# The end of a hybrid gMLP and differential-attention layer: output tiles in six PSUM banks issued ahead of the last block's transposes

## The reference, cut to what matters

```python
h = rms_norm(x, norm_w) * (1 + scale(c)) + shift(c)
u_a, v_a, z_a, q_b, k_b, v_b, z_b = split(h @ w_in)           # 7 x 512 columns
a_out = u_a * (tril(w_s) @ rms_norm(v_a) + b_s) * silu(z_a)   # chunks of 128 positions, 4 groups
q, k = rope(rms_norm(q_b)), rope(rms_norm(k_b))               # 8 heads of 64
o = (softmax(q1 @ k1.T) - lam * softmax(q2 @ k2.T)) @ v_b     # causal, 4 head pairs, v of 128
b_out = rms_norm(o, subln_w) * (1 - lam_init) * silu(z_b)
x = x + gate(c) * (concat(a_out, b_out) @ w_out)              # (2048, 1024) per core
```

## Time and profile before

| | us |
|---|---|
| median of 3 runs | 522.16 |
| lowest, highest of the 3 | 520.88, 527.08 |
| the profiled execution, its own time | 526.04 |
| its span, the slowest core (core 4) | 524.6 |
| spans of the other cores | 514.8 to 523.1 |

### The profile page before, as it was taken

How to read it: one execution, slowest core, us unless ns; L and a number is a source line. 1 busy time by engine, 2 the same in 40 slices (tenths; PEclk the granted TensorE clock), 3 DMA queues, 4 the chain that set the end, 5 groups by cost and what they waited for, 6 DMA issues and landing times.

```text
span 524.6 us, 9798 instructions; the slowest of 8 cores (514.8 to 524.6 us)
## 1 busy us (share of the span) xinstructions
PE 445.6 (85%) x3104; PEld 217.6 (41%) x3104; DVE 334.7 (64%) x761; ACT 299.2 (57%) x402; POOL 88.6 (17%) x118
## 2 busy tenths in 40 slices
PE   0037679899999999999998999979997999999396
PEld 0002224344443444444445555445554555555242
DVE  1246732682775468888873767788558757868732
ACT  1066456545554227777767666666778778677100
POOL 1113440000671000000001112222222222122100
PEclk9997869899999999999999999979998999999879
DMA  8999978007624300021021122194140131011013
GB/s 200 251 308 257 311 240 180 0 1 131 167 87 139 121 1 2 1 47 36 1 81 41 42 81 60 62 282 202 47 156 2 39 100 67 22 62 42 40 63 139
DMA packets 15606, 53.90 MB, mean 103 GB/s; under 512 B 2242, under 2 KB 2626, under 8 KB 14660
## 3 DMA queue, kind: packets, MB, share of 16 engines
q1 hardware_dynamic: 13924, 45.36, 26.0%
q0 software_dynamic: 1152, 7.50, 8.3%
q10 hardware_dynamic: 480, 0.41, 0.3%
HBM read 50.29 MB, written 8.39 MB: 112 GB/s over the span
## 4 chain that ended last, share of the span: by engine, by line
PE 60%; DVE 11%; DMA 9%; issue 7%; ACT 6%; POOL 5%; DVEq 0%; SPq 0%; ACTq 0%; POOLq 0%
PE psum L647 15%; PE psum L470 13%; PE psum L1049 8%; PE psum L927 7%; DMA sb_WO<-w_adaT 5%; PE psum L897 5%; ACT sb_cs L910 3%; DMA sb_kT<-xT 3%; PE psum L1015 3%; POOL sb_cs L915 3%; DVE sb_F L984 3%; DVE sb_F L943 1%; PE psum L677 1%; PE psum L675 1%; PE psum L667 1%
## 5 line engine op out<-in xcount | busy, mean ns | idle before, releaser
L910 ACT ACTIVATE sb_cs<-psum,sb_small 128x1024 bf16<-128x1024 f32 x144 | 150.9, 1113 | 58.6 <-PE psum L897 55.2
L927 PE MATMUL psum<-sb_vB,sb_cs 128*128 128x129 bf16 x1088 | 89.5, 226 | 9.7 <-DVE sb_F L943 5.2
L927 PEld LDWEIGHTS psum<-sb_vB,sb_cs 128*128 128x128 bf16 x1088 | 64.4, 100 | 40.5 <-issue 40.1
L470 PE MATMUL psum<-sb_W,sb_hT 128*128 128x512 bf16 x256 | 65.8, 420 | 17.5 <-ACT sb_hT L466 15.4
L915 POOL TENSOR_TENSOR sb_cs<-sb_cs,sb_constb 128x256 bf16<-128x256 bf16 x64 | 44.5, 697 | 213.3 <-ACT sb_cs L910 208.7
L647 PE MATMUL psum<-sb_hT,sb_W 128*128 128x512 bf16 x280 | 65.8, 379 | 0.0
L897 PE MATMUL psum<-sb_qT,sb_kT 64*128 64x256 bf16 (+1 forms) x576 | 56.4, 274 | 6.9 <-ACT sb_cs L910 4.7
L470 PEld LDWEIGHTS psum<-sb_W,sb_hT 128*128 128x128 bf16 x256 | 26.4, 105 | 56.2 <-issue 34.1
L357 DVE SCALAR_TENSOR_TENSOR sb_F<-sb_WO,sb_F 128x1024 f32<-128x1024 f32 x24 | 30.2, 1257 | 30.5 <-DMA sb_WO<-w_adaT 22.0
L647 PEld LDWEIGHTS psum<-sb_hT,sb_W 128*128 128x128 bf16 x280 | 27.3, 98 | 30.0
L436 PE MATMUL psum<-sb_vnA,sb_constb 128*128 128x512 bf16 x32 | 11.9, 507 | 30.5 <-ACT sb_vnA L429 30.5
(11 more groups left out here) (114 smaller groups left out, 548.4 us busy)
## 6 DMA issues: line engine op xcount, KB each, us to landing
sb_WO<-w_adaT SPq DMA_DIRECT2D x24, 512.0 KB, 8.1
sb_W<-w_in POOLq DMA_DIRECT2D x5, 1024.0 KB, 9.9
sb_W<-x SPq DMA_DIRECT2D x8, 512.0 KB, 4.4
sb_cs<-w_out SPq DMA_DIRECT2D x8, 512.0 KB, 3.4
sb_hT<-x SPq DMA_DIRECT2D x8, 512.0 KB, 12.0
out<-sb_hT SPq DMA_DIRECT2D x8, 512.0 KB, 2.6
out<-sb_W SPq DMA_DIRECT2D x6, 512.0 KB, 2.8
sb_qT<-xT SPq DMA_DIRECT2D x4, 512.0 KB, 23.4
```

Of the source, the lines that this page charges most:

```text
L470: pe(lambda E: E.matmul(PS(bank), lhsT=hT[:, kc, 128 * tt:128 * (tt + 1)], rhs=wsl[slot][:, kc, :], start=(kc == 0), stop=(kc == KC - 1)), ...
L910: act(lambda E: E.activation(out=et, in_=psum[:, X:X + 2, :], func=AF.Exp, bias=negM, scale=0.125), reads=[pb[X], pb[Y], b_lam], writes=[b ...
L927: pe(lambda E, u=u, j=j, c=c, i=i: E.matmul(psum[:, j, 256 * c:256 * c + 129], lhsT=et[:, c, QB * u + 128 * j:QB * u + 128 * (j + 1)], rhs ...
```

## The change

It replaces the closing loop. First the one waiting post is recorded. The list of banks becomes [2, 3, 4, 5, 6, 7, 0, 1]. The tasks of block 3 are recorded down to its last fin_head, until its transposes stand at the front of fillq. They are taken out, and the six output tiles that are left of earlier blocks are recorded on TensorE, in banks 2 to 7. Only then come the transposes, in bank 0. The posts follow in this order: those of the first three of the six tiles, the two copies of the transposes, those of the other three. The four tiles of block 3 follow in banks 1, 2, 3 and 4, two by two with their posts as before. The number of operations of each kind and the stores are as they were; nothing is added or left out.

```diff
@@ -1131,7 +1131,7 @@
     def fill_one():
         it = fillq.pop(0)
         kind, run, wt = it[0:3]
-        bank = FB[fb_ctr[0] % 2]
+        bank = FB[fb_ctr[0] % len(FB)]
         fb_ctr[0] += 1
         posts.append(run(bank))
         if kind == "u":
@@ -1176,18 +1176,32 @@
             fill_one()
         if (last or (gs > 0 and jq >= 6 and kp == 3)) and fillq and len(posts) < 2:
             fill_one()
-    s = NS + 1
-    while due or fillq or posts or taskq:
-        now[0] = s
-        run_posts()
+    now[0] = NS
+    run_posts()
+    FB[:] = [2, 3, 4, 5, 6, 7, 0, 1]
+    fb_ctr[0] = 0
+    while not (fillq and fillq[0][0] == "tr"):
         while taskq:
             taskq.pop(0)()
-            run_due(s)
-        run_due(s)
+        run_due(10 ** 9)
+    tr = fillq.pop(0)
+    lead = min(6, len(fillq))
+    for k in range(lead):
+        fill_one()
+    early = posts[0:3]
+    rest = posts[3:]
+    del posts[:]
+    fillq.insert(0, tr)
+    fill_one()
+    for fn in early + posts + rest:
+        fn()
+    del posts[:]
+    run_due(10 ** 9)
+    while fillq or posts:
+        run_posts()
         for k in range(2):
-            if len(posts) < 2 and fillq:
+            if fillq:
                 fill_one()
-        s += 1
 
     P.emit()
     for bb in b_xr:
```

## The result

| | before | after |
|---|---|---|
| median, us | 523.13 (4 runs, 520.88 to 527.08) | 513.11 (4 runs, 512.21 to 514.7) |
| ratio to before, 95% interval | | 0.984 (0.980 to 0.988) |
| profiled execution: own time, span | 526.04, 524.6 | 513.64, 512.6 |

The medians and ratios from here on leave out executions in which one die (cores 0 to 3 or 4 to 7) ran longer at a lower granted clock.

A forecast was written before the change was run, and what follows sets the result against it. The prediction took TensorE's 6.79 us hole before block 3's transposes, plus slow matmuls behind it, as the bound. An ending 9.4 us earlier, less 0.5 for stores, takes 8.9 off 522.16: 513.3 us, range 510.0 to 517.0.

The forecast's parts named there:

- Idle time and TensorE's order: Ahead of block 3's transposes: six tiles take 10.38 us without bank waits, ending at 502.21; the 6.79 us hole disappears.
- The chain on VectorE: Block 3's add, squares, norm and eight L984 on VectorE keep their order and end at 498.64 in both versions.
- First on VectorE: The change's phrase for block 3's chain on VectorE; claimed to move nothing, only the TensorE work beside it moves.
- The start of the ladder: Block 3's first add, opening the closing adds and stores, starts at 505.61 instead of 515.01, set by VectorE, not TensorE.
- core 4's rows may stand for all: All cores do the same work, so the slowest, core 4 at 524.6 us, was taken to represent all eight.
- The stores: At the end, stores come closer together and delay the first half-tile store by 0 to 1.7 us; 0.5 was taken.
- One of its own signs of being wrong: In the closing adds and stores: the first store taking over 3 us would show the prediction wrong.
- the second rival: Closing stores queue up fully, first one 1.7 us late instead of 0.5: gain 7.7, time 514.5 us; chance 0.06.
- The clock: Behind the end of attention TensorE stays at 2.4 GHz throughout; 0.81 over two tiles would cost 0.7 us.
- The first rival: Granted clock 0.81 from the start of the tail: gain 6.5 us, time 515.7 us; chance 0.15.
- The total: Whole kernel: gain 8.9 us off the 522.16 us median gives 513.3 us, 1.7% less; chance 0.61.
- The fifth rival: Clock falls to 1.2 GHz at the end of attention and stays there: slower than before, 523.8 us; chance 0.03.

The follow-up runs named there:

- Experiment 1: Kernel before plus 28 throwaway matmuls filling the idle time ahead of block 3's transposes, six tiles left behind them: 518.03 us, ratio 0.996 to the kernel before.
- experiment 6: Changed kernel with all six adds behind the copies of the transposes instead of three ahead of them: 517.87 us in a single execution, tail 29.1 us.
- experiment 7: Changed kernel with own buffers for second halves, five tiles ahead, four adds ahead of the copies; timed twice: 509.83 and 511.34 us, ratios 0.978 and 0.980.
- lead2: Changed kernel with two tiles ahead of the transposes instead of six: 516.84 us, ratio 0.992 to the kernel before.
- halves: Changed kernel with a separate buffer and semaphore for the second half of each of the last two row tiles: 510.34 us, ratio 0.981 to the kernel before.
- best_again: Second timing of the changed kernel with own buffers for second halves, five tiles ahead and four adds ahead of the copies: 511.34 us, ratio 0.980.

## Why the prediction was right

**Idle time and TensorE's order.** Right. Six tiles fit into the hole with no wait for a bank, and the transposes start 12.05 us behind the copies L943 (502.21 - 490.15 = 12.06 by the sum). Experiment 1 gives the idle time 5.2 us and the clock 2.5 of the 7.7 us.

**The chain on VectorE.** Right: 8.49 us in both. "First on VectorE" moved nothing.

**The start of the ladder.** The first add of block 3 started at 499.37 + 2.67 - 0.69 = 501.35, which is 15.61 us behind the copies, against 15.46 by the sum. VectorE set it, as forecast, and experiment 6 showed so. The 0.15 is the step between adds, 0.66 us here (2.67 for four) and not 0.60. The term of this step, a ladder that starts 9.4 us earlier, measured 24.86 - 15.61 = 9.25 against core 4 of the kernel before. But "core 4's rows may stand for all" was not quite so. Its ladder starts latest of the eight and is the shortest: 24.86 and 7.11 us, where the medians are 24.3 and 7.6. By the medians the ladder starts 8.7 us earlier. The sum of start and ladder is about the same (31.97 against 31.9), so the forecast lost nothing by it. One slip has no effect either: behind block 3's first tile only three are left, not four, so TensorE ends at about 510.2 by the prediction's own rows and not at 511, which is the 20.07 us measured.

**The stores.** This is the term that was mis-sized. From the first add's start to the last one's end the ladder took 510.10 - 501.35 = 8.75 us instead of 7.11. So 1.6 us were lost on these two cores, and 8.6 - 7.6 = 1.0 us in the medians of the eight, where the prediction took 0.5; its upper bound was 1.7. One of its own signs of being wrong came true here: the first store of the ladder took 3.4 us to land, against 2.0 before, and over 3 us was the sign. The two waits of adds were to be 2.2 us each and were 3.52 and 2.55, and TensorE ended 4.3 us ahead of the last add instead of 2. The prediction preferred the low end because a store 2.1 us behind a 512 KB one had taken 2.01 us all the same. Here two 512 KB stores are issued 2.0 and 0.6 us ahead of it (at 500.14 and 501.55, the ladder's about 502.1), and the DMA engines are busy nearly all the time until 504.5 (core 2; columns as before):

```profile
501.00:504.50 3.50, 3.50 (x18) 1.57 (x16) 1.04 (x2) 0.00 (x0) 0.00 (x0) 1.00 0.93 366
```

Over the same stretch the share is 0.92 to 0.93 on the other seven cores. Experiment 4 takes these two stores out, and 1.1 us come back. That is the mechanism of the second rival, which had a chance of 0.06 and a gain of 7.7 us. The gain in the tail is 9.25 - 1.64 = 7.6 us, 7.7 in the medians, and not 8.9; it is 7.5 us by the mean of the core spans and 8.2 us by the ratio of the runs.

**The clock.** Right: 1.00 through all tiles, in the first 20 us behind the copies L943 on all eight cores. The first rival, and with it the rule of the Trainium skill, page "TensorE: Matmul & The Clock Gate", Part 1, would have had 0.81 here with all eight cores at dense matmuls. Over the 24 us behind the last copies the clock was 1.00 on all eight cores of warm_hole too, with matmuls nearly throughout. This case doesn't bear the rule out as one that holds for every such stretch.

**The total.** 513.3 against 513.11 us is closer than the steps deserve, and that is luck. The gain of 8.9 us was taken off 522.16, the median of three runs. The 32 executions of the kernel before in the later comparisons have a mean of 521.3 us and 15 of the changed kernel one of 513.2, a gain of 8.1. So the forecast began 0.8 us too high and took off 0.8 us too much. Of the tail alone, 522.16 - 7.6 would have been 514.5 us.

**The fifth rival** named the clock as what could turn the change round. In the changed kernel, where TensorE goes on without a gap, it did not fall before the last tile was done. Experiment 2 shows how near that is: with only two tiles ahead the remaining 3.3 us of idle time bring the slow clock back.

## What to carry to other kernels

Work that is ready should stand ahead of a transpose or matmul that waits for a long chain on another engine, in as many banks as it takes to fill the whole wait. Filling half of it here kept the idle 3.3 us and the slow clock, and brought less than two thirds of the gain (4.9 of 7.7 us of tail). Then look at what comes last next: two halves of a tile that share one buffer for an add and a store cost 3.8 us here, more than any reordering of the adds. When several changes of 1 to 4 us are compared on eight cores, compare them by a stretch that begins where the code begins to differ, since the slowest core's arrival there scatters by more. Where only whole times are at hand, the mean over the cores' spans tells more than the slowest core: it showed 3.8 and 3.5 us in experiment 7, where the two comparisons of medians gave 3.3 and 1.7.

## What the runs showed of the hardware that was not expected

- 3.3 us without matmuls, behind dense work and ahead of dense work, brought the clock down on eight of eight cores (experiment 2). On core 6 it fell only after TensorE had begun again: the transposes at 494.50 still ran at full speed (0.61 us), the tiles behind them did not. It was so on cores 0 and 4 too; on the other five the transposes were slow already (1.01 us). With the gap filled down to 0.3 us it stayed at 1.00.
- The 0.81 level stood in the tail of the kernel before, on tiles behind the slow stretch (511.3 to 514.4 us on core 4). Six of the eight cores had it in windows of 1 us, from 21 us behind the copies at the earliest; cores 2 and 3 stayed at 1.00. No core had it in the first 20 us of the changed kernel or the first 24 us of warm_hole, although dense work ran there without the long gap. No core had it in lead2 either, which has a slow stretch too. What brings it was not tried.
- Where no add waits for a store, the tail is nearly the same on all cores (22.98 to 23.09 us in halves, 22.5 to 22.9 in best_again); with the ladder in it, it spreads by 0.5 to 1.4 us in the three profiles of the changed kernel.
